# Fewer places for the modulation chunks, and another order of sums and squares behind a residual

## The reference, cut to what matters

```python
ada = silu(c) @ w_ada[l] + b_ada[l]              # 6 x 1024 numbers per layer
sh1, sc1, g1, sh2, sc2, g2 = split(ada, 6)
u = h * (1 + sc1) + sh1
y = mixer(u)                                     # layer 0, 1: attention and mLSTM
h = layer_norm(ALPHA * h + g1 * y)
u = h * (1 + sc2) + sh2
y = (silu(u @ w1) * (u @ w3)) @ w2               # layer 2, 3: a 3-tap causal conv before silu
h = layer_norm(ALPHA * h + g2 * y)
```

## Time and profile before

| | |
|---|---|
| median of 3 runs | 3757.86 us (3754.81 to 3767.63) |
| the profiled execution, its own time | 3762.52 us |
| its span in the profile | 3760.3 us |
| mean granted TensorE clock | 0.965 |
| TensorE busy | 3566.2 us (95%) |
| VectorE, ScalarE, GpSimd busy | 1556.9, 1385.2, 1466.3 us |
| 16 DMA engines, queue of the weights | 34.5% |

### The profile page before, as it was taken

One profiled execution on the slowest core, in us unless ns is written; L12 is line 12 of the kernel. 1 busy time (PEld: TensorE's weight loads), 2 busy tenths in 40 slices (PEclk: granted clock), 3 DMA queues, 4 the chain that ended last, 5 costly groups with the idle time before them and its releaser, 6 DMA issues.

```text
span 3760.3 us, 39657 instructions
## 1 busy us (share of the span) xinstructions
PE 3566.2 (95%) x16304; PEld 2817.2 (75%) x16304; DVE 1556.9 (41%) x2130; ACT 1385.2 (37%) x2241; POOL 1466.3 (39%) x785
## 2 busy tenths in 40 slices
PE   7999999998999999999899999988889999999999
PEld 5887667777888788766687788876567887777887
DVE  4426564354442333665435444245535211443220
ACT  4444444223232344444322323245542223543221
POOL 2333333543554333333344355433125444224543
PEclk9999999998999899999999999988899999999999
DMA  6333211444553334321154455422015333213332
GB/s 206 107 101 118 56 45 53 138 133 124 167 170 109 103 101 124 101 56 45 54 143 129 135 167 160 121 70 79 6 53 158 104 95 90 71 51 90 95 95 73
DMA packets 566978, 385.30 MB, mean 102 GB/s; under 512 B 13598, under 2 KB 504302, under 8 KB 566798
## 3 DMA queue, kind: packets, MB, share of 16 engines
q1 hardware_dynamic: 564574, 379.56, 34.5%
q10 hardware_dynamic: 2224, 3.21, 0.3%
HBM read 379.25 MB, written 2.10 MB: 101 GB/s over the span
## 4 chain that ended last, share of the span: by engine, by line
PE 82%; DVE 7%; ACT 6%; POOL 2%; issue 1%; DMA 1%; SPq 0%; ACTq 0%; DVEq 0%; POOLq 0%
PE ps L174 81%; POOL wlo L144 2%; ACT whi L140 2%; ACT L136 1%; PE ps L178 1%; DVE ST L158 1%; DVE H L152 1%; DVE mq L152 0%; DVE np L144 0%; ACT sxb L136 0%; DVE sp L152 0%; DVE ACC L152 0%; DMA W<-in_w_ada 0%; ACT xr L136 0%; SPq L171 0%
## 5 line engine op out<-in xcount | busy, mean ns | idle before, releaser
L144 POOL TENSOR_TENSOR wlo<-raw,whi 128x1024 fp32r<-128x1024 f32 (+1 forms) x540 | 1282.2, 2384 | 1978.8 <-ACT whi L140 1978.5
L174 PE MATMUL ps<-UH,whi 128*128 128x512 f32 x2656 | 1073.2, 404 | 36.0 <-ACT UH L140 16.2
L174 PE MATMUL ps<-UH,wlo 128*128 128x512 f32 x2656 | 1052.2, 396 | 24.7 <-POOL wlo L144 24.7
L174 PE MATMUL ps<-UL,whi 128*128 128x512 f32 x2656 | 1048.6, 395 | 0.0
L140 ACT ACTIVATE whi<-raw 128x1024 fp32r<-128x1024 f32 (+1 forms) x540 | 545.3, 1022 | 383.7 <-PE ps L174 183.6
L174 PEld LDWEIGHTS ps<-UH,whi 128*128 128x128 f32 x2656 | 508.2, 191 | 167.4 <-ACT UH L140 26.6
L174 PEld LDWEIGHTS ps<-UH,wlo 128*128 128x128 f32 x2656 | 508.0, 191 | 146.7 <-POOL wlo L144 36.3
L174 PEld LDWEIGHTS ps<-UL,whi 128*128 128x128 f32 x2656 | 507.1, 191 | 108.7 <-DVE UL L144 2.2
L152 DVE SCALAR_TENSOR_TENSOR ACC<-raw,SM,ACC 128x512 f32<-128x512 f32 x308 | 354.1, 1150 | 20.4 <-DVE fg L144 0.5
L174 PE MATMUL ps<-GH,whi 128*128 128x512 f32 x704 | 275.7, 392 | 0.0
L174 PE MATMUL ps<-GL,whi 128*128 128x512 f32 x704 | 274.1, 389 | 0.0
(11 more groups left out here) (332 smaller groups left out, 4244.2 us busy)
## 6 DMA issues: line engine op xcount, KB each, us to landing
raw<-in_w_in SPq DMA_DIRECT2D x168, 512.0 KB, 4.2
raw<-in_w SPq DMA_DIRECT2D x120, 512.0 KB, 5.1
raw<-in_ada_w SPq DMA_DIRECT2D x96, 512.0 KB, 4.8
raw<-in_w_ada SPq DMA_DIRECT2D x80, 512.0 KB, 4.6
raw<-in_ffn_w_gate SPq DMA_DIRECT2D x44, 512.0 KB, 3.8
raw<-in_ffn_w_up SPq DMA_DIRECT2D x44, 512.0 KB, 3.9
raw<-in_ffn_w_down SPq DMA_DIRECT2D x32, 512.0 KB, 3.9
raw<-in_ev_w_in SPq DMA_DIRECT2D x20, 512.0 KB, 4.3
```

What stands on the lines that cost most here:

```text
L144: return self.e.tensor_tensor(o, a, b, op).then_inc(*self.done(*keys))
L174: m = self.e.matmul(o, l, r, start=start, stop=stop)
```

## The change

Two things, on the engines' programs alone; no operation is added or left out.

First, 22 pairs of fill calls go, 17 of them among the 220 that do something: the two in the attention of layer 1 at P=0, one at the first product pair of each gating, the one ahead of the last tile of each residual, and the three at the start of each feed-forward (m=0 twice, m=1 once). All later chunks move one place further with each of them, so that call 219 now lies at m=17 of layer 2's feed-forward and no longer at m=8.

Second, behind a residual: VectorE makes the last tile of H (and `Hc`) before it adds the squares of tile 6 (`dve_add(NT-2)`), the squares of the last tile go to a tile of their own (`UF` tile 7) and wait for no addition, TensorE takes the columns in the order H tile 7, squares of tile 7, N2, and `s1` behind them all; VectorE subtracts `s1` from all three first tiles only behind the factor.

```diff
 (pe_norm)
-        p.wait_ge(*on("dve", "p2", nid))
-        columns(4, N2, not means)
-        if means:
             p.wait_ge(*on("dve", "Hc", nid, NT - 1))
-            p.mm(o[:, :], ones, H[:, NT - 1, :], False, True, ("s1", nid))
             columns(0, H[:, NT - 1, :], False)
         p.wait_ge(*on("act", "sq", nid, NT - 1))
-        columns(4, N3, False, ("c2", nid))
+        columns(4, UF[:, NT - 1, :], not means)
+        p.wait_ge(*on("dve", "p2", nid))
+        columns(4, N2, False, ("c2", nid))
+        if means:
+            p.mm(o[:, :], ones, H[:, NT - 1, :], False, True, ("s1", nid))
 (act_sq)
-        if m > 1:
+        if 1 < m < NT - 1:
             a.wait_ge(*on("dve", "add", nid, m - 1))
-        a.af((N3 if m else N2)[:, :], H[:, m, :], ACT.Square, ("sq", nid, m))
+        a.af(UF[:, m, :] if m == NT - 1 else (N3 if m else N2)[:, :], H[:, m, :], ACT.Square, ("sq", nid, m))
 (dve_factor)
-        for kt in beside[:1]:
-            dve_again(v, nid, kt)
...
-        for kt in beside[1:]:
+        for kt in beside:
             dve_again(v, nid, kt)
 (pe_residual, dve_residual)
-            if fill:
+            if fill and m < NT - 1:
                 pe_fill(p)
...
             if m == NT - 1 and sums != "turned":
                 beside()
-                dve_add(v, nid, NT - 2)
...
+        if sums != "turned":
+            dve_add(v, nid, NT - 2)
 (attention, both engines)
-            if 0 < P + lay:
+            if P:
                 pe_fill(p)
 (gating)
-            pe_fill(p)
+                pe_fill(p)
 (feed-forward)
-        for m in range(FT):
-            pe_fill(p)
-            if m == 0:
-                pe_beside_norm(p, nid, [x + (LIN4,) for x in (one(0), two(0), one(1))])
+        pe_beside_norm(p, nid, [x + (LIN4,) for x in (one(0), two(0), one(1))])
+        for m in range(1, FT):
+            if m > 1:
                 pe_fill(p)
-                continue
-            if m > 1:
                 pe_lin(p, [one(m)], NT, UH, UL, None, LIN4)
             pe_fill(p)
             pe_lin(p, [two(m)], NT, UH, UL, None, LIN4)
```

More of the change, by code:

```diff
@@ L1398, in dve_attention @@
                 scores(2 * P + 1)
-            if 0 < P + lay and P < 13:
+            if 0 < P < 13:
                 dve_fill(v)
@@ L2056, in branches @@
         def branches(m):
-            dve_fill(v)
+            if m:
+                dve_fill(v)
             times(("wb", lay, m), ("gb", lay, m), T["sg"][g_slot(m, 1)])
```

## The result

| | before | changed |
|---|---|---|
| median | 3761.38 us, 4 runs (3754.81 to 3767.63) | 3724.02 us, 4 runs (3711.54 to 3731.72) |
| profiled execution, own time | 3762.52 us | 3731.72 us |
| its span | 3760.3 us | 3729.7 us |
| mean granted TensorE clock | 0.965 | 0.968 |

The account below looks back on a forecast made before the run. TensorE, 82% of the chain that ended last, bounds the kernel; only its idle or lower-clock time can be won. Terms sum to -25.0 us: 3762.5 to 3737.5 profiled, 3733 against the median of 3757.9; range 3722 to 3748.

Parts of the forecast that it names:

- Norm n1: Norm behind r0: H's last tile made earlier and s1 no longer ahead of the columns, -3.7 us.
- Norms n2 to n4: Later norms with means: column matmuls no longer wait behind s1, -1.0 us each, -3.0 together.
- Norms n6 to n8: Squares norms without s1: N2's columns now behind the last squares' columns, +0.9 us each; upper bound 0.9 + 2.4 behind a wlo.
- Starts of f0 and f1: Feed-forward starts, layers 0 and 1: w3's chunk m=1 split earlier, behind the silu of m=0; -3.7 and -2.7 us.
- all five places stall alike: Slower rival: the first fill's raw buffer comes free late, so all five places stall anew; +10 us, 3770, chance 0.04.
- f2's start and its nine steps: Layer 2's feed-forward: earlier split at its start, -2.2 us; nine more steps with fills at 1.1 us each, +9.9.
- Attention of layer 1: Waits at P=1 and P=2 and slow matmuls go, since weight chunks come within the look-ahead; -9.1 us, later steps nothing.
- Gating: Layer 1's gating: w_b of m=1 loads early, shrinking TensorE's 7.75 us wait; -6.5 us at lower clock, -8.9 at full.
- r2: Residual r2: the column at m=7 that waited 3.18 us for VectorE comes at m=6, without slow matmuls; -4.7 us.
- r1 and r3: These residuals each lose one column group, about 1 us of TensorE, to later stages; -2.0 us together.
- the clock comes back too: Rival: the lower clock may not come behind shortened stalls at f0, f1 and gating; 7 us more, 3726, chance 0.22.
- The change does nothing: Rival: the stalls had another cause, so only the moved fills and squares norms count; +12.6 us, 3770, chance 0.02.

Follow-up runs that it names:

- norms_only: The kernel before with only the new order behind a residual, every fill call kept: 3761.29 us, ratio 0.9999.
- fills_only: The change without the new order behind a residual, so only the fill calls move, against the kernel before: 3726.54 us, ratio 0.9913.
- attention_ahead: The kernel before, no fill moved, with ScalarE's and GpSimd's splits in layer 1's attention reaching one chunk further (4 instead of 3): 3751.22 us, ratio 0.9970.
- attention_only: The kernel before with only the two fill calls at P=0 of layer 1's attention taken away: 3740.17 us, ratio 0.9949.
- two_calls_f0: The kernel before with two fill calls fewer in layer 0's feed-forward (m=20 and m=21), all other calls kept: 3741.29 us, ratio 0.9949.
- squares_old_order: The change with the three squares norms (n6, n7, n8) back in the old order: 3722.30 us, ratio to the kernel before 0.9895.

## Why the prediction was right, and where it was not

The direction and the range held, 3724 against 3733 us forecast, within 3722 to 3748, and so did the mechanism of its larger terms: modulation chunks ahead of a weight chunk hold TensorE up. The second half of the change did not do what the prediction credits it with, and a part of the agreement is luck: one step gave 6.7 us more than said, which outweighs the gains at n2 to n4 that did not come and the squares norms that cost more. By its own steps:

- *Norm n1, -3.7*: the stage moved by -4.4 and -6.2, but the number agrees by luck and the cause is another. The step credited the new order, in the stretch from the sums to the columns' result; that stretch gave 1.95 us (2.59 in the second profile), and the rest lies ahead of it, in r0, for which the sum has no term. norms_only shows -0.1 for the order alone, fills_only -4.5 for the removed calls alone. That the fill "was over before" H's last tile was true and beside the point: norms_only, with the call and in the new order, waits for the last square behind ScalarE's three splits and their loads. The price was also read from a chance. Up to n1 attention_ahead, attention_only and two_calls_f0 run the same program as before. Where VectorE's addition began 0.07 or 0.02 us ahead of GpSimd's `wlo` it took 0.69 us, and the stretch 6.48 and 7.62; where it began 0.02 us behind, 2.88 and 10.00, as in the kernel before (0.04 us, 2.86, 9.06).
- *Norms n2 to n4, -1.0 each*: -1.6 or -0.8 at n2, where kernels without an edit there show -1.1, so no gain is shown; then about 0 and 0. At n3 the addition met a `wlo` (2.14 us), and at n4 the columns ran at the lower clock.
- *Norms n6 to n8, +0.9 each*: +0.9, +1.9, +1.7. Mis-sized: the row that priced it was at the full clock, and at n7 and n8 the same columns run at the lower one. The dearer bound, GpSimd's `wlo` in the way, came up once, at n6 of norms_only (+2.3).
- *Starts of f0 and f1, -3.7 and -2.7*: -4.3 and -2.0 (second profile -5.2 and -4.6). Right, and the clock came back only in some executions. In f1 there was a new wait at m=2, one of the prediction's own signs of being wrong, but of 0.7 us only. That all five places stall alike is refuted: f0 has the same long instructions (`GL` 2.39 us, the fill's 2.67) and no such wait behind them. *f2's start and its nine steps*, -2.2 + 9.9: +7.6, to the tenth, and by its parts too (-2.5 up to m=2, +10.1 behind).
- *Attention of layer 1, -9.1*: **-15.8**, the largest miss, and it sits in one sentence, "Later steps have short exponentials; I take nothing there, with 2 us to either side". The wait at the last product (3.62 + 1.85 us) stood in the trace of before and has the same origin as those at P=1, modulation chunks ahead of a weight chunk, three of them here. It was not looked for, since no call was taken away near it; the calls taken away far ahead of it moved the column call there. Up to the last `qk` copy, P=1 and P=2 with it, the stage gave 8.9 of the 9.1 (8.1 in the second profile).
- *Gating, -6.5 at the lower clock, -8.9 at the full one*: -8.2. The lower clock did come behind the wait for `wlo` (2.01 us), but for seven matmuls only (1836.7 to 1839.8, granted clock 0.50), and it was over before the next product; `w_b` of m=1 was loaded early, as the step says.
- *r2, -4.7*: -5.9. *r1 and r3, -1.0 each*: as forecast.
- What the profiles do not hold: the medians differ by 35 to 37 us, the profiles by 31 to 32. The last section has a stretch that may be a part of it.

The rival "the clock comes back too" (3726) is the nearest in time, and at the gating part of it happened; but most of what was missing was the unseen wait. "The change does nothing" falls with every row. What two_calls_f0 adds to the prediction's theory is its other half: the change works through how many modulation chunks lie between two weight chunks, and that is set by the places and by the count modulo five. As much as 20 of its 36 us can be had by moving the count by two, in a place where nothing ever waited, even though that move makes a new wait of 8.9 us at f2's start.

What stays open: whether each of the other calls has to go for its part of the gain (the three at each feed-forward start, the ones at the end of a residual) was not tried apart.

## What to carry to other kernels

When side work shares an in-order pipeline, its cost at a place is the number of its pieces that lie within the look-ahead and in the buffers there; write down that sequence for every place at which the main work waits, before and after an edit, also where nothing was edited. A wait can vanish through a shift made far away, and another can come by the same shift. Test the two halves of such a change apart: here reordering gained nothing, neither with the side work in its place nor with it moved off (3726.5 us without the new order, 3724.0 and 3726.9 with it), and moving the side work off gained all.

## What the runs showed of the hardware

- A VectorE instruction over one tensor of SBUF (`ACC<-raw,SM`, 0.48 us alone) waits for a running GpSimd instruction as much as one over two: 2.59 us beside a `wlo` of 2.53.
- Which of the two starts first decides, and hundredths of a microsecond can settle it. Of an addition with both inputs in SBUF and a `wlo` that began 0.02 us apart, the addition was first in attention_only (the first fence) and took 0.69 us, and `wlo` 2.89 in the place of its usual 2.35; in two_calls_f0 (the second) `wlo` was first, and the addition took 2.88. Both programs are the same up to there. So a stall of this kind in one profile need not be in the next.

```profile
843.93 0.69 DVE L144 TENSOR_TENSOR np<-np,np 128x512 f32<-128x512 f32 x1
843.95 2.89 POOL L144 TENSOR_TENSOR wlo<-raw,whi 128x1024 fp32r<-128x1024 f32 x1 [5.78 <-ACT whi L140]
```

```profile
840.74 2.35 POOL L144 TENSOR_TENSOR wlo<-raw,whi 128x1024 fp32r<-128x1024 f32 x1 [5.74 <-ACT whi L140]
840.76 2.88 DVE L144 TENSOR_TENSOR np<-np,np 128x512 f32<-128x512 f32 x1
```

- One stretch has two speeds for the same work. In layer 2's mixer, where the DMA queue is nearly idle in the window shown and TensorE waits for VectorE again and again, the profile of squares_old_order shows a granted clock of 0.95 in the window where the changed kernel has 0.86 (the fences below, in this order), and from n4 to r4's last H tile it took 8.2 us less, with no edit in or near it. The windows lie at the same time and not at the same work, so the whole stage is the fairer measure: a mean clock of 0.94 against 0.90. The profiles of the four kernels with two fills in r1 and r3 had the faster form too, all others the slower one. What chooses is open. Runs of the change differ by 20 us (3711.5 to 3731.7 us, mean clock 0.974 to 0.968); that this stretch is 8 of them is not shown, since both profiled executions of the change have the slower form.

```profile
2600.00:2700.00 100.00, 87.39 (x328) 53.44 (x327) 52.02 (x82) 59.90 (x73) 13.25 (x32) 0.95 0.02 6
```

```profile
2600.00:2700.00 100.00, 88.17 (x294) 50.62 (x293) 54.20 (x85) 57.63 (x70) 9.11 (x32) 0.86 0.00 0
```
